# Layer 0 of a two-layer transformer with retrieved experts: the second latent tile's attention and output projection placed behind the first latent tile's key search

## The reference

```
def parallel_mixers(h, hc, ...):
    parts, parts_c = split(h @ w_in), split(hc @ w_in)
    o_m = softmax_attend(q_m, k_m_all, v_m_all)          # 8 heads
    o_d = diff_attend(q_d, k_d_all, v_d_all, lam)        # 4 heads, two maps each
    return merge_groups(o_m, o_d) @ w_out, (the same for the context tokens, on context keys)

def peer_ffn(x):
    q = (x @ peer_wq).reshape(T, 8, 2, 128)              # 8 heads, two half keys
    s = einsum('thcd,ckd->thck', q, peer_subkeys)        # 128 scores for each half
    sv, si = top_k(s, 16)
    top_s, pos = top_k(all 16*16 sums of sv, 16)         # 16 experts for each head
    eidx, gate = (si[0]*128 + si[1])[pos], softmax(top_s)
    act = gelu(einsum('ted,td->te', u[eidx], x)) * gate  # u, v: 16384 experts of width 1024
    return einsum('te,ted->td', act, v[eidx])

x = x + g1 * y ;  x = x + g2 * peer_ffn(norm(x))
```

## Time and profile before

| | |
|---|---|
| median of 3 runs (lowest, highest) | 2674.01 us (2672.07, 2674.81) |
| the profiled execution | 2667.46 us |
| its span, first to last instruction | 2665.3 us |
| mean granted PE clock in it | 0.902 |
| PE, DVE, ACT, POOL busy | 78%, 69%, 43%, 36% |
| moved by DMA | 969.74 MB, mean 364 GB/s |
| chain that ended last | PE 34%, DVE 24%, DMA 21%, ACT 12%, issue 7% |

### The profile page before, as it was taken

The page is one execution under the profiler, slowest core; times in us unless marked ns, Lnnn a source line. Parts: engine busy times, 40 slices in busy tenths (PEclk is TensorE's granted clock), DMA queues, the critical chain, the costliest instruction groups (busy, mean ns, idle before and its releaser), DMA issues.

```text
span 2665.3 us, 25899 instructions
## 1 busy us (share of the span) xinstructions
PE 2085.1 (78%) x6680; PEld 1069.7 (40%) x6680; DVE 1850.8 (69%) x4482; ACT 1150.3 (43%) x3035; POOL 958.5 (36%) x916
## 2 busy tenths in 40 slices
PE   6997778879898888777677978769877887667775
PEld 2455434534454445333323333334543444333322
DVE  0146976975678769988876656554588686877775
ACT  2123483462377644434454333432245664433332
POOL 1012243333333333444445444430133433345542
PEclk9998899889899999888988998889888998899888
DMA  8479989989898899999999999996499999999997
GB/s 336 128 270 350 389 322 373 395 314 391 326 392 317 307 385 352 364 417 420 405 422 396 420 419 416 405 390 240 165 413 380 415 365 390 416 384 420 421 407 317
DMA packets 206904, 969.74 MB, mean 364 GB/s; under 512 B 17308, under 2 KB 69048, under 8 KB 108472
## 3 DMA queue, kind: packets, MB, share of 16 engines
q0 software_dynamic: 123648, 855.69, 79.6%
q1 hardware_dynamic: 83128, 112.56, 12.3%
HBM read 967.14 MB, written 1.05 MB: 363 GB/s over the span
## 4 chain that ended last, share of the span: by engine, by line
PE 34%; DVE 24%; DMA 21%; ACT 12%; issue 7%; POOL 1%; SPq 0%; POOLq 0%; DVEq 0%; ACTq 0%
DMA EXPERT<-in_peer_uv,FIX 20%; PE VS L964 14%; PE PA L824 10%; DVE EXPERT L1574 8%; DVE ACC L1584 2%; PE PA L852 2%; DVE SCR L1200 2%; PE PB L954 2%; ACT L1148 1%; ACT L1096 1%; PE PB L892 1%; ACT WEI L1150 1%; PE VS L782 1%; ACT DIAG L1155 1%; ACT HT L1053 1%
## 5 line engine op out<-in xcount | busy, mean ns | idle before, releaser
L964 PE MATMUL VS<-EXPERT,DIAG 128*128 128x512 f32 x2304 | 1205.0, 666 | 303.0 <-ACT DIAG L1155 302.5
L659 POOL DMA_INDIRECT EXPERT<-in_peer_uv,FIX x768 | 887.8, 1156 | 1163.7 <-PE VS L964 770.9
L1574 DVE CUSTOM_DVE_ANT_0 EXPERT<-EXPERT,H 128x1024 f32<-128x1024 f32 x768 | 924.2, 1223 | 324.6 <-DMA EXPERT<-in_peer_uv,FIX 314.3
L964 PEld LDWEIGHTS VS<-EXPERT,DIAG 128*128 128x128 f32 x2304 | 466.0, 213 | 908.9 <-issue 485.1
L1148 ACT ACTIVATE GEL<-DOT 128x1 f32<-128x1 f32 x768 | 155.2, 202 | 1024.2 <-DVE DOT L1574 1023.4
L824 PE MATMUL PA<-WT,HT 128*128 128x512 f32 (+2 forms) x720 | 298.5, 562 | 17.1 <-ACT HT L1053 7.8
L1584 DVE SCALAR_TENSOR_TENSOR ACC<-EXPERT,WEI,ACC 128x1024 f32<-128x1024 f32 x192 | 246.0, 1281 | 38.6 <-ACT WEI L1150 38.6
L1155 ACT ACTIVATE DIAG<-IDN,WEI 128x128 f32<-128x128 f32 x576 | 231.3, 401 | 71.3 <-PE VS L964 53.7
L1150 ACT ACTIVATE WEI<-GEL,GATE 128x1 f32<-128x1 f32 x768 | 226.3, 295 | 25.0
L954 PE MATMUL PB<-HT,WT 128*128 128x128 f32 (+1 forms) x1280 | 204.4, 321 | 17.2 <-issue 14.5
L954 PEld LDWEIGHTS PB<-HT,WT 128*128 128x128 f32 x1280 | 191.6, 215 | 44.8 <-issue 35.1
(11 more groups left out here) (146 smaller groups left out, 1681.7 us busy)
## 6 DMA issues: line engine op xcount, KB each, us to landing
EXPERT<-in_w_ada POOLq DMA_DIRECT2D x48, 1024.0 KB, 13.2
WT<-in_peer_wq SPq DMA_DIRECT2D x80, 512.0 KB, 14.9
WT<-in_w_in SPq DMA_DIRECT2D x48, 512.0 KB, 10.4
WT<-in_w_out SPq DMA_DIRECT2D x40, 512.0 KB, 8.6
EXPERT<-in_peer_uv,FIX POOLq DMA_INDIRECT x768, 11.4
WT<-in_w_in SPq DMA_DIRECT2D x16, 384.0 KB, 10.3
WT<-in_w_in SPq DMA_DIRECT2D x16, 288.0 KB, 5.9
WT<-in_mla_wq_up SPq DMA_DIRECT2D x4, 512.0 KB, 8.7
```

The lines of the kernel that those rows point to most:

```text
L659: pool.indirect_dma_start(out=EXPERT[:, j, :], out_offset=None, in_=a["peer_uv"], in_offset=bass.IndirectOffsetOnAxis(ap=FIX[:, par, j:j + ...
L964: ins = nc.tensor.matmul(VSUM[n][:, :], DIAG[:, i, :], EXPERT[:, j, D + n * W:D + (n + 1) * W], start=first, stop=last_one)
L1574: nc.vector.tensor_tensor_reduce(out=EXPERT[:, j, 0:D], in0=EXPERT[:, j, 0:D], in1=H2[:, b % HB, :], scale=1.0, scalar=0.0, op0=ALU.mult, ...
```

## The change

It is made in layer 0. Before, both latent tiles went through attention one after the other, then through one output projection and one key search with both tiles as the moving operand, of which heads 0 and 1 and most of head 2 stood in the first `weave`. After, latent tile 0 goes through attention, its own output projection and six heads of the key search alone (heads 0 to 5, three of them begun in the first `weave`). Latent tile 1's attention, its own output projection and the key search come behind: heads 6 and 7 for both tiles together, then heads 0 to 5 for tile 1 alone. They lie in the second `weave` (blocks 1 and 2), the third and the fourth (block 3). The front of layer 1, that before was spread over slot 96 of block 2 to slot 120 of block 3, has its place behind the last picks, in block 3 alone. `order_of` says where a head's experts lie in its block (for tile 1: heads 6, 7, 0 to 5).

```
-    if not (g == LAT and l == 0 and t == 0):
-        out.append(("gates", l, g, t))
-    return out + [("hnorm", l, g, t), ("heads", l, g, t)]
+    return out + [("gates", l, g, t), ("hnorm", l, g, t), ("heads", l, g, t)]
...
+ALONE = {(0, CTX): PH, (0, LAT): 6, (1, LAT): PH}
+def order_of(l, g, t):
+    n = 0 if t == 0 else ALONE[l, g]
+    return [*range(n, PH), *range(n)]
+def pick(l, g, heads):
+    out, prev = [], None
+    for n, head in enumerate([*heads, None]):
+        cur = head and (*head, n % 2)
+        out += [("pick", l, g, prev, cur), ("more", l, g, prev, cur)]
+        if prev and len(prev[1]) > 1:
+            out += [("also", l, g, prev, 1), ("then", l, g, prev, 1)]
+        prev = cur
     return out
+def pick_apart(l, g):
+    n = ALONE[l, g]
+    return (pick(l, g, [(h, (0,)) for h in range(n)]),
+            pick(l, g, [(h, BOTH) for h in range(n, PH)] + [(h, (1,)) for h in range(n)]))
...
-    rest = (attention(0, CTX, 1) + outward(0, CTX, (1,)) + pick(0, CTX, (1,)) + front(0, LAT, BOTH)
-            + attention(0, LAT, 0) + attention(0, LAT, 1) + outward(0, LAT, BOTH))
-    picks = pick(0, LAT, BOTH)
-    plan += weave(plan, first[4:] + rest + picks[:10], stream_of(0) + stream_of(1, 0, SLOTS - AHEAD))
+    rest = attention(0, CTX, 1) + outward(0, CTX, (1,)) + pick_apart(0, CTX)[1] + front(0, LAT, BOTH) + attention(0, LAT, 0)
+    alone, others = pick_apart(0, LAT)
+    plan += weave(plan, first[4:] + rest + outward(0, LAT, (0,)) + alone[:6], stream_of(0) + stream_of(1, 0, SLOTS - AHEAD))
+    joint = 2 + 4 * (PH - ALONE[0, LAT])
+    rest = alone[6:] + attention(0, LAT, 1) + outward(0, LAT, (1,)) + others[:joint]
+    plan += weave(plan, rest, stream_of(1, SLOTS - AHEAD) + stream_of(2, 0, SLOTS - 2 * AHEAD))
+    plan += weave(plan, others[joint:joint + 4], stream_of(2, SLOTS - 2 * AHEAD))
     fronts = front(1, CTX, THREE, queries=False) + front(1, LAT, (0,), keys=False)
-    plan += weave(plan, picks[10:], stream_of(1, SLOTS - AHEAD) + stream_of(2, 0, SLOTS - 2 * AHEAD))
-    plan += weave(plan, fronts[:4], stream_of(2, SLOTS - 2 * AHEAD))
-    plan += weave(plan, fronts[4:], stream_of(3, 0, SLOTS - RING))
+    plan += weave(plan, others[joint + 4:] + fronts, stream_of(3, 0, SLOTS - RING))
     plan += stream_of(3, SLOTS - RING)
...
-                at = slice(h * TOPK, (h + 1) * TOPK)
+                nth = order_of(l, g, t).index(h)
+                at = slice(nth * TOPK, (nth + 1) * TOPK)
...
-                dve.wait_ge(idx_ready[t], 8 * (b // 2) + h + 1)
+                dve.wait_ge(idx_ready[t], PH * (b // 2) + nth + 1)
```

More of the change, by code:

```diff
@@ L120, in outward @@
     return out
[L123 to L130, removed]
-    return out
+ALONE = {(0, CTX): PH, (0, LAT): 6, (1, LAT): PH}
[10 more added lines that the diff above has]
+        prev = cur
+    return out
+def pick_apart(l, g):
+    n = ALONE[l, g]
+    return (pick(l, g, [(h, (0,)) for h in range(n)]),
+            pick(l, g, [(h, BOTH) for h in range(n, PH)] + [(h, (1,)) for h in range(n)]))
 def holds(s):
@@ L157, in splits_pick @@
 def splits_pick(s):
-    return s[0] in ("pick", "more") and s[3] > 0 and len(s[4]) > 1
+    return s[0] in ("pick", "more") and s[3] is not None and len(s[3][1]) > 1
 def mingle(first, second):
@@ L191, in picks_of @@
 def picks_of(stage):
-    if stage[0] not in ("more", "then") or stage[3] == 0:
+    if stage[0] not in ("more", "then") or stage[3] is None:
         return []
-    _, l, g, h, ts = stage
-    return [blocks_of(l, g)[ts[0]] * SLOTS + TOPK * (h - 1)]
+    _, l, g, (h, ts, r), _ = stage
+    t = ts[0] if stage[0] == "more" else stage[4]
+    return [blocks_of(l, g)[t] * SLOTS + TOPK * order_of(l, g, t).index(h)]
 def weave(placed, background, stream):
@@ L269, in make_plan @@
     plan += [("adae", 0, 1), start[2], ("adat", 0, 1), ("mod", 0, 1)] + start[3:]
-    attend, leave, first = attention(0, CTX, 0), outward(0, CTX, (0,)), pick(0, CTX, (0,))
+    attend, leave, first = attention(0, CTX, 0), outward(0, CTX, (0,)), pick_apart(0, CTX)[0]
     plan += mingle(attend[:-2], modulation(0, (2, 3, 4))) + [("mod", 0, 2)]
@@ L288, in make_plan @@
     keys, attend, leave = front(1, LAT, (1,), queries=False), attention(1, LAT, 0), outward(1, LAT, (0,))
-    first, picks = pick(1, LAT, (0,)), pick(1, LAT, (1,))
+    first, picks = pick_apart(1, LAT)
     g1, sh2, sc2 = products(1, 2), products(1, 3), products(1, 4)
@@ L587, in pieces @@
                 w, (c0, n), ks = a["w_out"][l], (stage[3] * W, W), (KP * stage[5], KP * stage[5] + KP)
-            elif kind == "pick" and stage[3] < PH:
-                v = a["peer_wq"][l].rearrange("(k p) n -> p k n", p=P)
-                return [(v[:, k:k + HP, stage[3] * HW:(stage[3] + 1) * HW], HP, HW) for k in range(0, KD, HP)]
+            elif kind == "pick" and stage[4]:
+                v, h = a["peer_wq"][l].rearrange("(k p) n -> p k n", p=P), stage[4][0]
+                return [(v[:, k:k + HP, h * HW:(h + 1) * HW], HP, HW) for k in range(0, KD, HP)]
             elif kind == "up":
@@ L925, in pick_ @@
             def pick_(stage):
-                _, l, g, h, ts = stage
+                _, l, g, prev, cur = stage
                 release()
-                if h == 0:
+                if prev is None:
                     pe.wait_ge(emptied_b, rb.n)
-                if h >= 1:
-                    pe.wait_ge(emptied_b, held[h - 1, 1])
+                else:
+                    h, ts, r = prev
+                    pe.wait_ge(emptied_b, held["queries", 1])
                     for t in ts:
@@ L934, in pick_, with key_query @@
                         for c in range(2):
[L935 removed]
+                            last = nc.tensor.matmul(bank[:, c * P:(c + 1) * P], QP[:, r, c, t * P:(t + 1) * P],
                                                     SKT[:, 2 * l + c, :], start=True, stop=True)
                         last.then_inc(filled_a, 1)
[L938 removed]
+                if cur is not None:
                     held["w"] = [head_piece() for k in range(0, KD, HP)]
[L940 removed]
+                    key_query(cur, 0)
             def more(stage):
[L943 to L945 removed]
+                cur = stage[4]
+                if cur is not None:
+                    key_query(cur, 1)
                     owed.append((filled_b, rb.n, KD // HP))
[L948 to L950 removed]
+            def key_query(cur, c):
+                h, ts, r = cur
                 mine = slice(ts[0] * P, (ts[-1] + 1) * P)
@@ L956, in key_query @@
                 last.then_inc(filled_b, 1)
-                held[h, c] = rb.n
+                held["queries", c] = rb.n
             def apply(no, i, j, first=False, last_one=False):
@@ L1118, in pick_, with key_query @@
             def pick_(stage):
-                key_query(stage, 0)
+                key_query(stage[4], 0)
             def more(stage):
[L1122 to L1130, removed]
+                _, l, g, prev, cur = stage
+                if prev is not None:
+                    gate_exps(prev[1][0])
+                key_query(cur, 1)
+            def key_query(cur, c):
+                if cur is not None:
+                    h, ts, r = cur
+                    mine = slice(ts[0] * P, (ts[-1] + 1) * P)
                     bank = from_b()
-                    nc.scalar.copy(QP[:, h % 2, c, ts[0] * P:(ts[-1] + 1) * P], bank[:, ts[0] * P:(ts[-1] + 1) * P])\
-                        .then_inc(emptied_b, 1)
+                    nc.scalar.copy(QP[:, r, c, mine], bank[:, mine]).then_inc(emptied_b, 1)
             def then(stage):
-                gate_exps(stage[4][0])
+                gate_exps(stage[4])
             def gate_exps(t):
@@ L1479, in pick_ @@
             def pick_(stage):
-                _, l, g, h, ts = stage
-                if h < PH:
+                _, l, g, prev, cur = stage
+                if cur is not None:
                     rb.next()
                     rb.next()
-                if h == 0:
-                    return
-                top(ts[0])
+                if prev is not None:
+                    top(prev[1][0])
             def more(stage):
-                _, l, g, h, ts = stage
-                if h > 0:
-                    experts(l, g, h - 1, ts[0])
+                _, l, g, prev, cur = stage
+                if prev is not None:
+                    experts(l, g, prev[0], prev[1][0])
             def also(stage):
-                top(stage[4][0])
+                top(stage[4])
             def then(stage):
-                _, l, g, h, ts = stage
-                experts(l, g, h - 1, ts[0])
+                _, l, g, prev, t = stage
+                experts(l, g, prev[0], t)
             def mark(ins):
```

## The result

The changed kernel took 2646.84 us (median of 4 runs, 2641.1 to 2653.47) beside 2673.04 us for the kernel before, a ratio of 0.9904 with a 95% interval of 0.9879 to 0.9928: 19 to 32 us faster. The forecast was 2648 us, or -26. In five more runs it took 2648.74 us, ratio 0.9907 (0.9886 to 0.9928).

A forecast was written before the change was run, and what follows sets the result against it. It took engines to bound stretch A and transfers stretch B. Terms of -58 (work out of A), +30 (added transfers) and +2 (end of block 0) gave -26 from 2674.01, so 2648 us, range 2620 to 2686.

The forecast's parts named there:

- A: Stretch to the end of the first weave, 240 slots, 816 us before; forecast to take 758 us.
- B: Stretch from the first weave's end to slot 120 of block 3, 712 us before; forecast to take 742 us.
- What bounds the kernel: A held up by engines (DMA share 0.93), B by transfers (share 0.99), with PE and DVE free for a quarter of B.
- Added transfers: 20 more weight pieces, 10.49 MB at 2.84 us a MB, all in B with nothing hiding them: +30 us.
- Work out of A: 1026 planner units of engine work leave A, worth 46 to 70 us; the middle taken, -58 us.
- floor of 733: Least time in us that A's transfers allow, at the saturated price of rows and a DMA share of 0.99.
- lower bound of 46: Least gain in us from the 1026 units leaving A, at 0.044 us a unit, from A and block 4.
- No loss for engines in B: The 1026 units moved into B stay hidden under transfers: 0 in the sum, up to 6 us in the range.
- End of block 0: Two qd projection parts before close where cq stood, 16 records taking 7.1 us: +2 us, bounded by 0 and 8.
- Scores' waits: PE waits for ACT's query copies before scores: nine new in B, 34 us of PE, hidden, costed at 0.
- The rest: After slot 120 of block 3, all as before, only shifted; no term in the sum.
- the signs that the prediction named: A done by about 995 us, share 0.97 or more; B about 742 us at 0.98 to 0.99, dots' waits below 148.9.

The follow-up runs named there:

- 1: Kernel before, with latent tile 1's layer 0 attention stages left out of A (565 planner units less): 2623.97 us, ratio 0.9831.
- 11: Kernel before, with most weight pieces of A loaded at an eighth of their bytes (22.6 MB less): 2673.04 us, ratio 0.9997.
- 4: Kernel before, with 20 pieces of weights in B loaded twice (9.6 MB more), engines' work unchanged: 2690.38 us, ratio 1.0063.
- experiment 2: Changed kernel, with latent tile 1's layer 0 attention stages left out of B: 2648.85 us, ratio 0.9917.
- 10: Changed kernel, with most weight pieces of A loaded at an eighth of their bytes (22.6 MB less): 2633.15 us, ratio 0.9865.
- 12: Changed kernel, with context tile 1's layer 0 attention left out of A (565 planner units less): 2625.3 us, ratio 0.9832.

## Why the prediction was right

The direction, the places and the net are as forecast. What holds each stretch up is shown by experiments; that the net agrees within 3 us is in part luck, since inside the term for A two errors cancel, and the one in B is made up for by blocks that the sum left alone.

- **What bounds the kernel.** Right, and shown: A by its engines (experiments 1 and 11), B of the kernel before by its transfers: 9.6 MB added alone cost 21 us there (4). That B took the moved attention almost free is experiment 2.
- **Added transfers, 29.8 us, all in B.** The bytes are exact: 980.26 MB, 92 pieces of `peer_wq`, 48 of `w_out`. B grew by 39 us in the mean of the profiles (41.5 in the first pair), so this term was 9 us short. B's DMA work grew by 48 us, not 30. The forecast counted the new pieces alone; B also carries the 4.1 MB that A had fetched ahead before, an estimated 10 us, and some 2 MB for the slots behind it. That this is why B was short is worked out from the bytes, and no run shows it by itself.
- **Work out of A, -58 us (-56 with the end of block 0).** A fell by 57 in the mean (50.7 in the first pair, whose changed profile has the longest A of eight). The number is right by two errors. The engines gain 70 us for the 1026 units (10), 0.068 a unit where I took 0.057, and a unit isn't one price: attention alone gave 0.087 (1). And I let A run down to the larger of two limits; it runs above both, at 757 to 766 us with an engines' limit of 746 and a floor of 733, which takes 11 to 19 back. (The lower bound of 46 in the sum should read 45, 1026 x 0.044; the middle stays 58.)
- **No loss for engines in B.** Nearly right for attention (4 us), but not for all of it: B with neither attention nor heavy pieces is 21 us shorter than with both, with either alone 4 and 9.
- **End of block 0, +2 us.** It was 4. Before, 15.6 us lay between the last slot product before `close` (673.75) and block 1's first dot (689.3); after, 19.7 (643.02 to 662.76), with 12 records of `qd` and a rotation in place of a copy. POOL sat 10.78 us instead of 7.61:

```profile
643.02 5.16 PE PA L845 x12
```

```profile
655.55 0.94 POOL L680 DMA_INDIRECT EXPERT<-in_peer_uv,FIX  x1 [10.78 <-DVE ACC L1606]
```

- **Scores' waits (L935 before, L957 after).** 14.2 us in 5 waits in B where I allowed 34 in nine. No run takes them away alone.
- **The rest.** From slot 504 to the first dot of block 4 the profile shows 159.3 us instead of 163.5; PE's clock was granted at 0.94 instead of 0.92 there. The sum had nothing there, and it is no scatter: four profiles with the order before show 163.5 to 164.6, ten with the order after 157.2 to 160.1. Its cause stays open. Blocks 4 and 5 are as they were (717.4 before, 715.7 after).

Of the first pair's 14 us: -50.7 + 41.5 - 4.2 - 1.7 is -15 to the last dot. The errors in A and B add up there, and this profile would have called the forecast 11 us too good. The runs say 24 to 26, but an execution of this kernel varies by 12 us.

Of the signs that the prediction named, A's were missed in this profile: it was done by 1003 us, not 995, at a share of 0.95, not 0.97. (In the other seven with the same A it was done by 993 to 1003 us, at 0.96 to 0.97.) B took 757 us, not 742, of which 4 us are where the rows ended it. B's share (1.00) and the dots' waits in B (122.8 us, between those of before in A and in B) were about as named.

On the Trainium skill's limit of about 358 GB/s for one core (DMA: Bandwidth & Descriptors, Where 436 GB/s comes from): the trace of the changed kernel has 377 in A and 403 in B over 757 us. So A's 359 GB/s before was no ceiling, as experiments 1 and 11 say by other means. This program runs on one core; no run here has a second core moving data beside it.

## What to carry to other kernels

- Moving work from a stretch that waits for engines to one that waits for transfers pays by the difference, and both sides can be estimated from the rows: busy shares say where, the shares of the queues what a MB costs at most. To learn which limit a stretch has, make its loads light: if nothing changes (11), the engines hold it; if removing engine work changes nothing (2), the transfers do.
- Near the crossing the time isn't the larger of the two limits. Here A lay at 757 to 766 us, 11 to 19 above its engines' limit of 746 and 24 to 33 above its transfers' floor, and in B taking one load away gave less than half its price, taking both away more than the sum. Where a forecast brings a stretch down to the crossing of its limits, it should stop above the larger one; here that was 1.5 to 2.6%.
- Transfers that run ahead shift time between windows. Compare the MB of the two windows before reading their times.
- One profile is one execution. A's length differed by 8 us among eight profiles of the same list; runs that leave a stretch as it is give its scatter for nothing.

## What was not expected of the hardware

- A DMA share of 0.99 to 1.00 in a window doesn't mean that bytes alone set the time: in B of the changed kernel it read 1.00, yet 20 pieces at an eighth of their bytes (9.2 MB less) gave 9 us instead of 26. The share then read 0.98, which looks full but leaves 15 of 748 us; the third digit counts.
- A MB of gathered rows has no fixed price. In A it was 2.62 us at a DMA share of 0.88 (11), 2.55 at 0.93 (before), 2.48 at 0.95 (after) and 2.45 at 0.98 (12), and in B before 2.43 at 0.99. The less full the window, the longer its packets are on record; 10, with 2.51 at 0.91, lies somewhat off that line.
